# A mixture-of-experts stage with fifteen weight slots instead of twelve, another order of places, and another order of work on ScalarE

## What is computed

```python
def hier_moe(h, w_rg, b_rg, w_re, b_re, w_gate, w_up, w_down):
    ...                                  # group by softmax, top 2 of its 4 experts, weights e_w
    combine = jnp.sum(jax.nn.one_hot(expert_id, MOE_EXPERTS, dtype=F32) * e_w[..., None], axis=-2)
    out = jnp.zeros_like(h)
    for e in range(MOE_EXPERTS):         # 16 experts, hidden width 512
        he = jax.nn.silu(h @ w_gate[e]) * (h @ w_up[e])
        out = out + combine[..., e:e + 1].astype(h.dtype) * (he @ w_down[e])
    return out

x = x + hier_moe(h2, ...)
x = x + jax.nn.sigmoid(x @ w_ple_gate[i]) * (p[i] @ w_ple_proj[i])
```

## Time and profile before

| | us |
|---|---|
| median of three runs | 1636.7 |
| the profiled execution | 1639.9 |
| its span, first to last instruction | 1638.1 |
| PE busy in the span | 1537.1 (94%) |
| POOL busy | 1270.2 (78%) |
| ACT busy | 720.8 (44%) |
| DVE busy | 712.8 (44%) |
| moved by DMA | 334.6 MB, mean 204 GB/s |

### The profile page before, as it was taken

The page is one execution under the profiler, slowest core; times in us unless marked ns, Lnnn a source line. Parts: engine busy times, 40 slices in busy tenths (PEclk is TensorE's granted clock), DMA queues, the critical chain, the costliest instruction groups (busy, mean ns, idle before and its releaser), DMA issues.

```text
span 1638.1 us, 22007 instructions
## 1 busy us (share of the span) xinstructions
PE 1537.1 (94%) x7044; PEld 1167.6 (71%) x7044; DVE 712.8 (44%) x1316; ACT 720.8 (44%) x887; POOL 1270.2 (78%) x1513
## 2 busy tenths in 40 slices
PE   7999999999999989899999989999999898899966
PEld 5777877788877868688788867878775465476625
DVE  3986844301037968834101067174555221212225
ACT  4544543544446554444444435546332223245423
POOL 7997898999999996869999988977663335368823
PEclk9999999999999999999999999999999999999987
DMA  6754454667765543535676655645365989889980
GB/s 220 219 167 121 136 154 142 208 212 222 214 200 168 151 145 116 154 109 167 215 217 207 190 175 155 200 140 165 116 222 213 378 291 349 334 301 341 383 329 26
DMA packets 95429, 334.62 MB, mean 204 GB/s; under 512 B 11136, under 2 KB 15760, under 8 KB 94256
## 3 DMA queue, kind: packets, MB, share of 16 engines
q1 hardware_dynamic: 90752, 314.34, 58.5%
q10 hardware_dynamic: 3440, 14.93, 2.6%
q0 software_dynamic: 1152, 4.19, 0.7%
HBM read 323.17 MB, written 21.78 MB: 211 GB/s over the span
## 4 chain that ended last, share of the span: by engine, by line
POOL 52%; PE 26%; issue 15%; DMA 3%; DVE 2%; ACT 1%; SPq 1%; POOLq 1%; DVEq 0%; ACTq 0%
POOL w_lo L1835 52%; PE bank L684 7%; PE bank L1191 5%; PE bank L1245 4%; PE bank L1188 3%; PE bank L1211 3%; DMA arena<-in_experts 2%; PE bank L1260 1%; DMA outputs_by_expert<-xn 1%; PE bank L1284 1%; POOLq L1830 0%; DMA raw<-outputs_by_expert,tiny 0%; PE bank L713 0%; PE bank L1231 0%; PE bank L1086 0%
## 5 line engine op out<-in xcount | busy, mean ns | idle before, releaser
L1835 POOL TENSOR_TENSOR w_lo<-raw,w_hi 128x256 fp32r<-128x256 f32 x1416 | 1066.6, 792 | 140.4 <-ACT w_hi L1421 139.6
L684 PE MATMUL bank<-w_hi,hT 128*128 128x512 f32 x2240 | 714.6, 400 | 33.5 <-POOL w_lo L1835 13.4
L1421 ACT ACTIVATE w_hi<-raw 128x1024 fp32r<-128x1024 f32 x356 | 377.1, 1059 | 523.9 <-DMA raw<-in_stream 261.2
L684 PEld LDWEIGHTS bank<-w_hi,hT 128*128 128x128 f32 x2240 | 415.8, 191 | 136.7 <-POOL w_lo L1835 21.0
L684 PE MATMUL bank<-w_lo,hT 128*128 128x512 f32 x1120 | 441.5, 394 | 0.0
L1842 POOL TENSOR_TENSOR w_lo<-arena,w_hi 128x1024 fp32r<-128x1024 f32 x80 | 189.5, 2386 | 155.2 <-ACT w_hi L1421 154.8
L684 PEld LDWEIGHTS bank<-w_lo,hT 128*128 128x128 f32 x1120 | 213.2, 190 | 47.0
L1421 ACT ACTIVATE w_hi<-arena 128x1024 fp32r<-128x1024 f32 x80 | 84.3, 1056 | 104.1 <-PE bank L1191 40.7
L995 PE MATMUL bank<-w_hi,mixT 128*128 128x512 f32 x352 | 111.7, 399 | 5.4 <-DVE mixT L2254 5.2
L684 PE MATMUL bank<-w_hi,mixT 128*128 128x512 f32 x288 | 91.5, 399 | 3.9 <-POOL w_lo L1835 2.5
L2246 DVE SCALAR_TENSOR_TENSOR arena<-bank,tiny,arena 128x256 f32<-128x256 f32 x44 | 21.1, 484 | 158.6 <-ACT arena L1577 143.7
(11 more groups left out here) (389 smaller groups left out, 1901.1 us busy)
## 6 DMA issues: line engine op xcount, KB each, us to landing
raw<-in_stream SPq DMA_DIRECT2D x356, 512.0 KB, 3.6
arena<-in_experts SPq DMA_DIRECT2D x192, 512.0 KB, 7.2
rows_by_expert<-in_blank ACTq DMA_DIRECT2D x56, 128.0 KB, 3.2
arena<-in_stream SPq DMA_DIRECT2D x10, 512.0 KB, 12.2
gates<-rows_by_expert SPq DMA_DIRECT2D x3, 1024.0 KB, 7.3
outputs_by_expert<-xn SPq DMA_DIRECT2D x3, 1024.0 KB, 7.9
bias_skewed<-bias_windows SPq DMA_DIRECT2D x4, 512.0 KB, 5.2
outputs_by_expert<-in_blank ACTq DMA_DIRECT2D x4, 512.0 KB, 4.5
```

Source lines behind the costliest of these rows:

```text
L684: mm = pe.matmul(LIN[t][:, :], lhs[:, a, k0 + k, t * P:(t + 1) * P], w[:, k, :], start=(k0 + k == 0 and n == 0), stop=(k0 + k == nk - 1 an ...
L1421: act.activation(w_hi[:, s, :], src, ACT.Copy).then_inc(s_hi, 1)
L1835: part = nc.gpsimd.tensor_tensor(w_lo[:, i, c], raw[:, i, c], w_hi[:, i, c].bitcast(F32), ALU.subtract)
```

## The change

Four things are changed, all in the expert stage.

1. The expert weights have fifteen slots: twelve in `arena` and, for s modulo 15 of 12 to 14, the three buffers `raw` of the front part. Their first use waits until the last front quarter has been split.
2. The rows gathered back at the end no longer land in `raw`, but in `gates[:, 1]` and in two parts of `logits`.
3. The order of places becomes W, P P W, P P W, P P, S S S S, P, P: the wide place of rank 0 is worked first.
4. In a paired place ACT makes no high parts ahead before its turned rows. It makes only those of the down quarters of a preceding place that is not paired (`needed`), reads out the turned groups of place p + 1, and makes high parts for at most two quarters beyond the place (`far=2`) before its `gated` activation.

```diff
-DEPTH = 12
+ARENA_SLOTS = 12
+DEPTH = ARENA_SLOTS + RING
...
-RANKS = (13, 12, 0, 11, 10, 1, 9, 8, 2, 3, 4, 5, 6, 7, 14)
+RANKS = (0, 13, 12, 1, 11, 10, 2, 9, 8, 3, 4, 5, 6, 7, 14)
...
-        back = [raw[:, 0, :], raw[:, 1, :], raw[:, 2, :], logits[:].rearrange("p h w -> p (h w)")[:, 0:D]]
+        back = [gates[:, 1, t, :] for t in range(TT)] + [logits[:].rearrange("p h w -> p (h w)")[:, 2 * t * D:(2 * t + 1) * D] for t in range(TT)]
...
         def slot(s):
-            at = TT * GLU * 2 + (s % DEPTH) * QK * QC
+            i = s % DEPTH
+            if i >= ARENA_SLOTS:
+                return raw[:, i - ARENA_SLOTS, :]
+            at = TT * GLU * 2 + i * QK * QC
             return arena[:, at:at + QK * QC]
...
+                elif s >= ARENA_SLOTS:
+                    sp.wait_ge(s_hi, FRONT_Q)
+                    sp.wait_ge(s_lo, FRONT_Q)
...
-            def ahead(s):
+            def needed(s):
+
+                for _ in range(split_before(s + 1) - hi.n):
+                    high()
+
+            def ahead(s, far=6):
 
                 for _ in range(split_before(s + 1) + (3 if s in WHOLE else 2) - hi.n):
-                    if hi.n >= ALL_SPLIT or SPLIT_AT[hi.n - FRONT_Q] > s + 6:
+                    if hi.n >= ALL_SPLIT or SPLIT_AT[hi.n - FRONT_Q] > s + far:
                         return
                     high()
...
-                ahead(last)
+                ahead(last, 2 if paired(p) else 6)
...
                 for p in range(POSITIONS):
-                    ahead(gate_up_at(p, 0, 0))
-                    hidden_split(p - 1)
-                    if not paired(p):
-                        gated(p, 0)
-                    rows_split(p + 1, 0)
-                    ahead(down_at(p - 1, 1, 1))
-                    rows_split(p + 1, 1)
...
                     if paired(p):
+                        hidden_split(p - 1)
+                        if p > 0 and not paired(p - 1):
+                            needed(down_at(p - 1, 1, 1))
+                        rows_split(p + 1, 0)
+                        rows_split(p + 1, 1)
...
                         rows_split(p + 1, 2)
                         rows_split(p + 1, 3)
                         gated(p, 1)
                         continue
+                    ahead(gate_up_at(p, 0, 0))
+                    hidden_split(p - 1)
+                    gated(p, 0)
+                    rows_split(p + 1, 0)
+                    ahead(down_at(p - 1, 1, 1))
+                    rows_split(p + 1, 1)
```

More of the change, by code:

```diff
@@ L1769, in experts_act @@
                 for p in range(POSITIONS):
-                    ahead(gate_up_at(p, 0, 0))
-                    hidden_split(p - 1)
-                    if not paired(p):
-                        gated(p, 0)
-                    rows_split(p + 1, 0)
-                    ahead(down_at(p - 1, 1, 1))
-                    rows_split(p + 1, 1)
-                    if p == LAST_AT:
-                        act.wait_ge(s_tr, tr.up())
-                        act.activation(last_T, TR[(tr.n - 1) % 2][:, 0:SEQ], ACT.Copy).then_inc(s_th, 1)
-                    if paired(p):
+                    if paired(p):
+                        hidden_split(p - 1)
[3 more added lines that the diff above has]
+                        rows_split(p + 1, 1)
+                        if p == LAST_AT:
+                            act.wait_ge(s_tr, tr.up())
+                            act.activation(last_T, TR[(tr.n - 1) % 2][:, 0:SEQ], ACT.Copy).then_inc(s_th, 1)
                         rows_split(p + 1, 2)
```

## The result

The changed kernel takes 1622.5 us (median of six runs, 1619.3 to 1628.9) against 1635.8 us for the kernel before on the same chip: ratio 0.992, 95% interval 0.989 to 0.994. That is 13.3 us less; 12.5 were forecast. The two profiled executions differ by more, 1638.1 and 1617.6 us of span, and the first thing to do is to see why. The lines are the spans and PE's first wait in the expert stage, before and after; its line number moves by 7.

The account below looks back on a forecast made before the run. The expert stage was taken as a balance of PE and DMA, losing time at changes from P to W. 22.8 - 4.4 - 0.9 - 1 - 1.5 - 2.5 = 12.5 us, median 1636.7 to 1624.2 us, range 1617 to 1633.

Parts of the forecast that it names:

- The cause: At changes from P to W, PE idles because ACT's program order puts a high part with an unlanded quarter before turned groups.
- What is taken away, 22.8 us: Places 1, 4 and 7: 16.6 us of PE waits for turned groups plus the slow clock behind them, together 22.8 us.
- Starts of W, 2.2 us each: At two W starts PE waits for read-out, high part and POOL's low part: 2.2 us each, 4.4 together.
- Opening, 0.9 us: At place 0, now wide, 1 MB of rows instead of 0.25 MB delays the start by 0.9 us, bounds 0 to 3.
- Start of S, 1 us: At place 9, two pairs cover high and low part: 0 if the quarter is there, 2.2 us if not; 1 taken.
- The third W ends at 1424 us; 56.7 MB follow at 363 to 390 GB/s: Late expert stage: PE ends the third W at 1424 us; the remaining 56.7 MB of transfers end between 1569 and 1580 us.
- Late waits, 1.5 us: In the late part, where PE and DMA limits are close, PE waits for quarters cost 1.5 us (0 to 5).
- Given back at the end, 2.5 us: The store of place 13 stands behind more quarters in SP's queue, costing 2.5 us (0 to 4).
- the 13 to 16 named as a sign: Sign in the profile after: the store of place 13 lands 13 to 16 us after its issue.
- The first W now stands at the opening, so two changes from P to W are left: W first leaves two P to W changes, each with a 2.2 us PE wait, 4.4 us together.
- rival A: Slots give no lead, only ACT's order acts: 9 us gained, 1627.5 us; chance 0.18.
- The rule on queues: At the end, engines alternate between queue rows, so deeper prefetch delays the store but not the gather: gather term 0, otherwise up to 4 us.

Follow-up runs that it names:

- e2: Only ACT's new order in paired places, against the kernel before; twelve slots and old place order stay: ratio 0.992, stage 385.1 us against 395.7.
- e7: Changed kernel with ACT making the high part of the next place's first quarter before the last two turned groups: ratio 0.989 against the kernel before, stage 375.0 us.
- e6: Changed kernel with the store of place 13 issued early, ahead of proj 0: ratio 0.990 against the kernel before, stage 379.9 us against the changed kernel's 380.1.
- e3: Only the fifteen slots and the gather's new buffers, against the kernel before; old orders of places and ACT: ratio 0.991, stage 382.1 us.
- e1: Only the order of places (W first), against the kernel before; twelve slots and old ACT order stay: ratio 1.000, stage 393.5 us.
- e5: Changed kernel without the fifteen slots, so W first and ACT's order only: ratio 0.995 against the kernel before, stage 388.0 us.
- e11: The changed kernel unaltered, measured and profiled once more on another chip: ratio 0.992 against the kernel before, stage 381.8 us.
- e4: Changed kernel without W first, so fifteen slots and ACT's order with the old place order: ratio 0.990 against the kernel before, stage 374.4 us.

## Why the prediction was right, point by point

**The cause.** Right. The wait of PE came from ACT's program order and from late quarters, and e2 shows that the order alone is worth 10.6 us with everything else as before.

**What is taken away, 22.8 us.** Right, and somewhat low. To X the changed kernel gains 15.5 us. Its new waits there are 0.71 + 2.24 + 2.25 + 1.62 + 0.20 = 7.0 us, so 22.5 us of the old loss are gone, and some 24 with the lower clock that follows one of them. I did not count the lower clock that lasted into two W places before: 0.91 on average for 2.6 us from 1366.4 us on and 0.80 for 3.1 us from 1433.9 us on, an estimated 0.9 us.

**Starts of W, 2.2 us each.** 2.24 and 2.25 us, by the chain that was summed, and e7 takes them away with it. Behind the first of them the clock fell, which the sum did not have: it was 0.65 on average for 4.4 us.

**Opening, 0.9 us.** 0.71 us, and 0.44 to 1.46 in other profiles.

**Start of S, 1 us.** 1.82 us in two waits. The two pairs cover high and low part, as I said, but the quarter lands late, which I held for the worse case.

**The third W ends at 1424 us; 56.7 MB follow at 363 to 390 GB/s.** It ends at 1420.34 us in the profile after, which is 4.9 us ahead at the stage's first row, so at 1425.2 in the times of before. What follows to the gather's issue is 139.56 us at 391 GB/s, 54.6 MB, with a DMA share of 1.01. The transfers go on beside the gather to about 1570 us: 149.66 us at 392 GB/s, 58.7 MB, 2 MB more than I had counted. They end at about 1575 us in the times of before, between the 1569 and 1580 of the forecast.

**Late waits, 1.5 us.** This term was in the wrong place. PE waits 1.77 us for a quarter (0.70 before), but behind X, beside the store and the gather. To X, PE waits for nothing behind the start of place 10, so the term was 0.

**Given back at the end, 2.5 us.** 1.1 us more to the gather's issue and 0.2 less to the weighing. The mechanism (quarters in front of the store) is shown by e6. The store landed in 11.7 to 12.9 us, a little under the 13 to 16 named as a sign. But what puts more quarters in front of it is W first beside the slots: with the slots alone (e3) it lands in 6.9 to 8.2 us, against 11.0 to 11.8 before, so deeper prefetch by itself gave 3.6 us there and took none back.

**The step that was wrong.** "The first W now stands at the opening, so two changes from P to W are left", with the first loss (8.6 us) booked as gained. The place order has no such gain: e1 is at 1.000, because the first S inherits a start behind P P, with 4.7 us of waits. And beside slots and ACT's order it costs 5.8 us between X and the gather for the 1.5 us that it gains to X. The total came out right because that gain was carried by the slots. I had given them almost nothing at the starts of W (4.7 against 4.4 us) and 3.5 us in all, the distance to rival A, while e3 measures 13.6 us of stage for them alone and e5 7.9 us beside the other two parts. So the total is luck as far as this split goes: two errors, a gain too many for W first and too few for the slots, cancelled. The sum did not test the split; the experiments did. A slip of 0.1 us stands in rival A as well: from 1425.61 + 3.4 to 1433.9 us it is 4.9, not 4.8.

**The rule on queues.** In e6, fourteen quarters are issued from 1.2 us behind the store on, and the gathers on the other queue land 8.0 to 11.9 us after their issues, against 7.2 to 8.2 in the changed kernel. The last gather, issued at 1567.8 us, lands at 1579.7, ahead of the quarter that SP issued at 1565.2, which lands at 1580.3. By the rule of the Trainium skill, page "DMA: Bandwidth & Descriptors", section "Queues, rings and completion order", rows of queues take turns, and the trace agrees: the gather shares the rate with the loads, but it does not stand behind all that was issued before. What I made of this rule for the store, that depth delays it, e3 does not bear out.

## What to carry to other kernels

When an engine's program is one list, look for a step that waits for a transfer ahead of a step that others wait for: here moving it was worth 10.6 us alone, and the same pattern came back at the end of the stage as soon as a load was moved. Deeper prefetch and a better order of work can cure the same wait, as here, so measure each alone before adding their gains. Moving expensive places ahead moves the transfer-limited part to the end, where the last store stands in its queue; put such a store ahead of loads that nobody needs yet, and then look for what stood behind those loads. A queue of its own for the store was not tried.

## What the runs showed of the hardware that I had not expected

Two waits of PE of the same length (2.24 and 2.25 us), behind the same kind of work, had different ends: the granted clock was 0.65 on average in the 4.4 us behind the first, so the lower level (1.2 GHz) for most of them, and 1.00 (2.4 GHz) behind the second (the windows in the first section). Nor was it the place: e11 repeats this pattern, but in e6, whose work up to there is the same, both waits (2.25 us each) were followed by 0.61 over 4.4 us. So a wait's price in clock was not to be had from its length alone.

Executions of the same front part differ by up to 16 us (1235.4 to 1251.5 us at the stage's first row), more than the whole effect of the change; on one chip alone it was 11.7 us (e2 and e4). What causes that was not tried.
